# Gate and up projections of two feed-forward layers by Strassen's identity: seven half-size products in place of eight

## The chip, the cores and the metric

The kernel runs on one core of one Trainium2 chip. The metric is the device time of one execution, in microseconds. Before the change the median of three runs is 2283.34 us (2282.11 to 2284.97).

## What is computed

512 tokens of width 1024 pass through two blocks. The first is a mixer (mLSTM and a spatial gate) and a mixture of 32 experts. The second has two layers, each a mixer (HGRN2 in layer 0, dilated attention in layer 1) and a feed-forward part. The change is in the feed-forward part of both layers:

```python
D_FF = ((8 * D_MODEL // 3 + 255) // 256) * 256      # 2816, that is 22 chunks of 128

def swiglu_ffn(u, w_in, w_down):
    gate, up = jnp.split(u @ w_in, 2, axis=-1)
    return (jax.nn.silu(gate) * up) @ w_down

        h = h + swiglu_ffn(rmsnorm(h, norm_ffn[layer]), ffn_w_in[layer], ffn_w_down[layer])
```

## The kernel before

**Precision.** Every large product is made of three: a number is split into a high part (what the fp32r type keeps of it) and a low part (the rest), and `product` (L576 to L580) adds high x high, high x low and low x high in one bank of PSUM. ScalarE makes the high parts by a copy, VectorE the low parts by a subtraction.

**Weights.** They stream through SBUF in units of 1 MB (128 partitions x 2048 floats). SyncE loads them into four buffers `raw`, in order. For unit n ScalarE writes `w_hi[n % 2]` (`split`, L1310; in the loops L1568) and VectorE `w_lo[n % 2]` (L1808; in the loops L2240). A unit of the gate/up projections holds, for each of the 8 chunks of the model width, 128 gate columns and 128 up columns. A unit of the down projection holds 4 chunks of the hidden width x 512 output columns.

**A feed-forward layer.** The residual stream `hs` lies transposed: 8 row blocks of 128 model rows x 512 tokens. `u_hi`, `u_lo` are `hs` times the norm's gain; the factor 1/rms per token is applied to the results, as the tile `rms`. There are 22 gate/up units. After the first 12 (`FA`) come six units of the down projection (`out_rows`), then the other 10 gate/up units and again six down units (`out_rows`, in the last layer `last_rows`). For one gate/up unit (`unit` inside `ffn`):
- TensorE makes the gate into bank 2s and the up into bank 2s+1, s = n % 2, each with 8 x 3 products of 128x128 (weights, stationary) and 128x512 (moving).
- VectorE multiplies gate by rms (L2422), ScalarE takes the SiLU (L1680), GpSimd multiplies by rms again (L2714, that is for up), VectorE multiplies by the up bank (L2425: `f_hid`), ScalarE takes the high part (L1683) and VectorE the low part (L2428) of the hidden chunk.

**Order.** Each engine has one queue, which is written out by hand and runs in that order; semaphores join them. Most of a pass is in a loop of four units a trip. `add_rows` (VectorE) and `norm_rows` (ScalarE) stand between the stages: they add the eight banks of a down projection to `hs` as they become complete, and make `u_hi`, `u_lo` and the squares for the next norm; GpSimd sums the squares (`add_squares`).

Of the kernel before, what the change touches and what calls it, by code (L numbers as in the profile page):

```python
# [15 lines left out]
P = 128  # L16
# [6 lines left out]
HALF = D // 2  # L23
NG = 8
# [15 lines left out]
FA = 12  # L40
# [33 lines left out]
def columns(*sizes):  # L74
    at, out = 0, {}
    for name, n in sizes:
# [11 lines left out]
                        ("n_mix", 2 * KC), ("n_ffn", 2 * KC), ("lb", 3 * KC), ("og", 1), ("levels", 8 * P))  # L88
P3_LATE, P3_FIRST = P3_COLS["spare"][0], P3_COLS["n_mix"][0]
FIRST_LEVEL = 11  # L90

# [26 lines left out]
def build(nc, x_in, weights_in, constants_in, phase1_in, phase2_in, phase3_in, out):  # L118
    with ExitStack() as ctx:
# [149 lines left out]
        sq = [place(f"sq{n}", [T], at_b + (24 + n) * KB2) for n in range(2)]  # L269
        sq_acc = place("sq_acc", [T], at_b + 26 * KB2)  # L270
# [34 lines left out]
        f_hid = [place(f"f_hid{n}", [T], at_a2 + (6 + n) * KB2) for n in range(2)]  # L305

# [94 lines left out]
        PROJ_ATTN = 4 * (HH // 2) + FC  # L401
# [82 lines left out]
        fin_root, fin_ready = sem("fin_root"), sem("fin_ready")  # L484
        block = ctx.enter_context(nc.Block())
# [84 lines left out]
        def _(pe):  # L570
# [373 lines left out]
            def norm(k):  # L944

                pe.wait_ge(n_acc, 6 * k)
                nc.tensor.matmul(bank[4][:], ones, sq_acc[:], start=True, stop=False)
                pe.wait_ge(n_sq, KC * k)
                nc.tensor.matmul(bank[4][:], ones, sq[1][:], start=False, stop=True).then_inc(n_sum, 1)
# [6 lines left out]
            def out_rows(n0, n_chunks, source, ready=None, bank_free=None, between=None):  # L956
# [3 lines left out]
                for half in range(2):  # L960
                    for q in range(per_half):
                        n = n0 + half * per_half + q
                        unit_wait(n)
                        for d in range(4):
                            if bank_free is not None and half == 0 and q == 0:
                                bank_free(d)
                            for k in range(4 if q else lead):
# [5 lines left out]
                                mm = product(bank[4 * half + d][:], w_hi[:, n % 2, w], w_lo[:, n % 2, w], hi, lo,  # L973
# [161 lines left out]
            def ffn(l, u0):  # L1135

                def unit(n, done, i=None):

                    def at(v):
                        return v if i is None else i * 4 + v  # L1140
                    s = n % 2
                    pe.wait_ge(hi_ready, at(nth(n) + 1))
                    pe.wait_ge(lo_ready, at(nth(n) + 1))
                    if not (l == 0 and done < 2 and i is None):
                        pe.wait_ge(f_prod, at(done - 1))
                    feature_chunk(bank[2 * s][:], s, 0, 1 + 2 * l if n == u0 and i is None else None).then_inc(proj_ready, 1)
                    feature_chunk(bank[2 * s + 1][:], s, 1).then_inc(unit_used, 1)

# [9 lines left out]
                pe.wait_ge(h_added, 4 + 24 * l)  # L1158
                for j in range(4):
                    unit(u0 + j, base + j)  # L1160
                with pe.Fori(1, FA // 4) as i:
                    for j in range(4):
                        unit(u0 + j, base + j, i)
                out_rows(u0 + FA, FA, lambda c: (hid2_hi[:, c], hid2_lo[:, c]), hidden_ready(0),
                         lambda d: pe.wait_ge(f_prod, base + FA - 1 + d // 2))
                pe.wait_ge(h_added, 12 + 24 * l)
                u1 = u0 + FA + 6
                with pe.Fori(0, 2) as i:
                    for j in range(4):
                        unit(u1 + j, base + FA + j, i)  # L1170
                for j in range(8, FC - FA):
                    unit(u1 + j, base + FA + j)
                if l == 1:
                    last_rows(u1 + FC - FA, FC - FA, hidden_ready(FA), lambda b: pe.wait_ge(f_prod, base + FC - 1 + b // 2))
                    return
                out_rows(u1 + FC - FA, FC - FA, lambda c: (hid2_hi[:, c], hid2_lo[:, c]), hidden_ready(FA),
                         lambda d: pe.wait_ge(f_prod, base + FC - 1 + d // 2))

# [120 lines left out]
        def _(act):  # L1299
# [5 lines left out]
            def split(n):  # L1305

                act.wait_ge(raw_landed[n % RAW], (AFTER_MOE if n >= U_HG else 0) + 16 * (nth(n) // RAW + 1))
                if n >= 2:
                    act.wait_ge(unit_used, n - 1)
                nc.scalar.activation(w_hi[:, n % 2], raw[:, n % RAW], ACT.Copy).then_inc(hi_ready, 1)  # L1310
# [220 lines left out]
            def square(k, c, wait_chunk):  # L1531
# [6 lines left out]
                nc.scalar.activation(sq[c % 2][:], hs[:, c], ACT.Square).then_inc(n_sq, 1)  # L1538
# [25 lines left out]
            def split_trip(n, i, per):  # L1564

                act.wait_ge(raw_landed[n % RAW], i * (16 * per // RAW) + (AFTER_MOE + 16 * (nth(n) // RAW + 1)))
                act.wait_ge(unit_used, i * per + (n - 1))
                nc.scalar.activation(w_hi[:, n % 2], raw[:, n % RAW], ACT.Copy).then_inc(hi_ready, 1)  # L1568
# [94 lines left out]
            norm_rows(1, U_HGO, 2, g_ffn[:, 0:KC], 0, 1)  # L1663

            def ffn(l, u0):
                base = l * FC

                def unit(n, chunk, slot, i=None):

                    def at(v):  # L1670
                        return v if i is None else i * 4 + v
                    if i is None:
                        split(n + 1)
                    else:
                        split_trip(n + 1, i, 4)
                    s = n % 2
                    if chunk == base and i is None:
                        root(1 + 2 * l)
                    act.wait_ge(f_scaled, at(chunk + 1))
# [1231 lines left out]
```

## Time and profile before

| | |
|---|---|
| median of the runs | 2283.34 us |
| the profiled execution, its time | 2283.39 us |
| its span in the trace | 2281.7 us |
| busy: TensorE, VectorE, ScalarE, GpSimd | 2093.5, 905.9, 667.4, 381.2 us |
| gate/up stretches | 1207 to 1342, 1409 to 1522, 1830 to 1965, 2032 to 2145 us |
| granted TensorE clock, mean | 0.973 |

PE is TensorE, PEld its weight loads, DVE VectorE, ACT ScalarE, POOL GpSimd, SP SyncE. Matmul records overlap, since they are pipelined, so the sum of their durations is more than the time in which TensorE is busy. A line can be that of a helper: L578 to L580 stand for all products.

### The profile page before, as it was taken

Reading aid. Unit: us, or ns where it says so; the run is one execution under the profiler, and the core shown is the slowest. Engines: PE = TensorE matmul, PEld = TensorE weight load, DVE = VectorE, ACT = ScalarE, POOL = GpSimd, SP = SyncE. Lnnn points to the kernel's source line nnn. Section 1 sums busy time; section 2 is a strip of 40 time slices with the busy share of each in tenths; the row PEclk is TensorE's granted clock in tenths of the full one; section 3 lists DMA queues with packets and bytes.
Section 4 is the critical chain, followed back from the end, with each engine's and each line's share of the span. In section 5 each row is a group of like instructions: output and inputs, shape, how many; then the busy total and the mean of one; then the engine's idle time right before and its main releaser. Section 6 shows DMA issues by size and latency. Waiting matters only on the chain.

```text
span 2281.7 us, 26227 instructions
## 1 busy us (share of the span) xinstructions
PE 2093.5 (92%) x10354; PEld 1555.0 (68%) x10354; DVE 905.9 (40%) x1168; ACT 667.4 (29%) x851; POOL 381.2 (17%) x364
## 2 busy tenths in 40 slices
PE   6997968777787779999999999999999999999998
PEld 5895833232232348888777888877889987888887
DVE  5536340000000026777754333336766234333332
ACT  3434211100101016666533221223222423221222
POOL 0000320000000004545521100102444001100100
PEclk9998979999999999999999999999999999999999
DMA  5230379999999971111212222232222322222220
GB/s 206 78 108 1 122 303 420 421 421 421 421 421 421 421 324 67 64 56 59 91 44 93 92 92 92 92 111 92 83 87 91 130 93 77 98 102 92 92 92 37
DMA packets 57658, 378.13 MB, mean 166 GB/s; under 512 B 8960, under 2 KB 9056, under 8 KB 13920
## 3 DMA queue, kind: packets, MB, share of 16 engines
q1 hardware_dynamic: 51120, 363.04, 40.6%
q0 software_dynamic: 6448, 13.82, 1.6%
q8 instruction: 65, 1.06, 0.2%
q14 instruction: 25, 0.20, 0.0%
HBM read 371.01 MB, written 15.26 MB: 169 GB/s over the span
## 4 chain that ended last, share of the span: by engine, by line
PE 67%; DMA 18%; DVE 7%; issue 5%; ACT 2%; SPq 0%; POOL 0%; DVEq 0%; POOLq 0%
PE bank L578 19%; PE bank L580 19%; PE bank L579 19%; DMA moe_w<-weights_in 17%; PE bank L840 3%; PE bank L863 2%; DVE o_tmp L2330 1%; DVE k_dec L2306 1%; PE bank L936 1%; PE bank L1259 1%; PE bank L706 1%; PE bank L1037 1%; PE bank L1049 1%; DVE ws L2315 0%; PE bank L1207 0%
## 5 line engine op out<-in xcount | busy, mean ns | idle before, releaser
L578 PE MATMUL bank<-u_hi,w_hi 128*128 128x512 f32 x1152 | 464.7, 403 | 0.7 <-issue 0.7
L580 PE MATMUL bank<-u_hi,w_lo 128*128 128x512 f32 x1152 | 456.6, 396 | 0.0
L579 PE MATMUL bank<-u_lo,w_hi 128*128 128x512 f32 x1152 | 456.4, 396 | 0.0
L1808 DVE TENSOR_TENSOR w_lo<-raw,w_hi 128x2048 fp32r<-128x2048 f32 x96 | 232.6, 2423 | 301.6 <-ACT w_hi L1310 301.3
L840 PE MATMUL bank<-moe_w,xe 128*64 128x512 f32 x1088 | 266.9, 640 | 90.0 <-DMA moe_w<-weights_in 86.3
L840 PEld LDWEIGHTS bank<-moe_w,xe 128*64 128x64 f32 x1088 | 92.7, 146 | 263.3 <-issue 263.1
L1310 ACT ACTIVATE w_hi<-raw 128x2048 fp32r<-128x2048 f32 x96 | 183.6, 1912 | 273.8 <-PE bank L580 272.8
L578 PEld LDWEIGHTS bank<-u_hi,w_hi 128*128 128x128 f32 x1152 | 217.2, 189 | 53.9 <-issue 3.5
L579 PEld LDWEIGHTS bank<-u_lo,w_hi 128*128 128x128 f32 x1152 | 217.4, 189 | 53.1 <-issue 2.4
L580 PEld LDWEIGHTS bank<-u_hi,w_lo 128*128 128x128 f32 x1152 | 217.1, 188 | 52.8
L578 PE MATMUL bank<-w_hi,u_hi 128*128 128x256 f32 (+1 forms) x640 | 192.4, 301 | 6.8 <-issue 6.8
L580 PE MATMUL bank<-w_hi,u_lo 128*128 128x256 f32 (+1 forms) x640 | 189.3, 296 | 0.0
L579 PE MATMUL bank<-w_lo,u_hi 128*128 128x256 f32 (+1 forms) x640 | 188.2, 294 | 0.0
L2714 POOL TENSOR_TENSOR f_gate<-f_gate,rms 128x512 f32<-128x512 f32 x44 | 56.9, 1294 | 569.2 <-ACT f_gate L1680 569.2
L2179 DVE SCALAR_TENSOR_TENSOR hid<-bank,slot_scale,gate 128x512 f32<-128x512 f32 x16 | 12.0, 751 | 324.1 <-PE bank L840 324.1
L863 PE MATMUL bank<-moe_w,hid_t 128*64 128x512 f32 x544 | 123.3, 596 | 15.0 <-ACT hid_t L1467 9.8
L578 PEld LDWEIGHTS bank<-w_hi,u_hi 128*128 128x128 f32 x640 | 121.7, 190 | 10.9 <-issue 8.0
L579 PEld LDWEIGHTS bank<-w_lo,u_hi 128*128 128x128 f32 x640 | 122.5, 191 | 3.0
L580 PEld LDWEIGHTS bank<-w_hi,u_lo 128*128 128x128 f32 x640 | 121.0, 189 | 3.2
L2425 DVE TENSOR_TENSOR f_hid<-f_gate,bank 128x512 f32<-128x512 f32 x44 | 30.3, 688 | 213.7 <-PE bank L580 213.7
L578 PE MATMUL bank<-hid_hi,w_hi 128*128 128x512 f32 x272 | 107.9, 397 | 0.1
L580 PE MATMUL bank<-hid_hi,w_lo 128*128 128x512 f32 x272 | 107.8, 396 | 0.0
(434 smaller groups left out, 2800.4 us busy)
## 6 DMA issues: line engine op xcount, KB each, us to landing
moe_w<-weights_in SPq DMA_DIRECT2D x204, 1024.0 KB, 25.1
raw<-weights_in SPq DMA_DIRECT2D x128, 1024.0 KB, 4.8
y_pairs<-pair_rows SPq DMA_DIRECT2D x4, 1024.0 KB, 7.8
res<-x_in SPq DMA_DIRECT2D x1, 2048.0 KB, 7.8
token_rows<-xn POOLq DMA_DIRECT2D x4, 512.0 KB, 3.4
v_rows<-vals SPq DMA_DIRECT2D x2, 1024.0 KB, 4.3
vals<-v_rows SPq DMA_DIRECT2D x2, 1024.0 KB, 8.0
out<-out_tile SPq DMA_DIRECT2D x4, 512.0 KB, 2.6
```

The source lines that it names most:

```text
L578: nc.tensor.matmul(out_ap, a_hi, b_hi, start=first, stop=False)
L579: nc.tensor.matmul(out_ap, a_hi, b_lo, start=False, stop=False)
L580: return nc.tensor.matmul(out_ap, a_lo, b_hi, start=False, stop=last)
L706: mm = nc.tensor.matmul(bank[4 + b // 2][:, at:at + VH], dec_at(j, b * P, b * P + P), vm[:, j, h * VH:h * VH + VH], start=b % 2 == 0 and j ...
L840: mm = nc.tensor.matmul(bank[2 + j // 2][rows, :], xe[:, c, rows], moe_w[2 * j + b][:, w], start=c == 0, stop=c == KC - 1)
L863: mm = nc.tensor.matmul(bank[5 + half][rows, :], hid_t[:, c, rows], moe_w[2 * j + b][:, w], start=c == 0, stop=c == 3)
L936: mm = nc.tensor.matmul(of_block(c, b), y_pairs[b][:, k, c * P:c * P + P], share_diag[:, k, b], start=False, stop=b == TB - 1 and k == 1)
L1037: mm = nc.tensor.matmul(bank[4 + n % 2][:, t], left, right, start=True, stop=True)
L1310: nc.scalar.activation(w_hi[:, n % 2], raw[:, n % RAW], ACT.Copy).then_inc(hi_ready, 1)
L1808: nc.vector.tensor_tensor(w_lo[:, n % 2], raw[:, n % RAW], w_hi[:, n % 2].bitcast(F32), ALU.subtract) \
L2425: nc.vector.tensor_tensor(f_hid[s][:], f_gate[s][:], bank[2 * s + 1][:], ALU.mult).then_inc(f_prod, 1)
L2714: nc.gpsimd.tensor_tensor(f_gate[n][:], f_gate[n][:], rms[:], ALU.mult).then_inc(f_gated, 1)
```

## The change

With A the weights of one unit and B the activations, both are cut in four. A's halves are 512 of the 1024 model rows (second index) and gate or up columns (first index); B's are the same model rows (first index) and 256 of the 512 tokens (second index). The form used is Winograd's variant of Strassen's identity, with seven products and fifteen sums:

S1 = A21 + A22, S2 = S1 - A11, S3 = A11 - A21, S4 = A12 - S2;
T1 = B12 - B11, T2 = B22 - T1, T3 = B22 - B12, T4 = B21 - T2 up to sign;
P1 = A11 B11, P2 = A12 B21, P3 = S4 B22, P4 = A22 T4, P5 = S1 T1, P6 = S2 T2, P7 = S3 T3;
U2 = P1 + P6, U3 = U2 + P7, U4 = U2 + P5;
C11 = P1 + P2, C12 = U4 + P3 (gate), C21 = U3 + P4, C22 = U3 + P5 (up).

Each P is 4 x 3 matmuls of 128x128 by 128x256 in its own bank. GpSimd makes the S sums, VectorE the T sums (once a layer, `add_pairs`) and the C and U sums (each unit); ScalarE and VectorE split every part in high and low; ScalarE copies P1 and P5 to SBUF. Parts have one buffer each (`part_hi`, `part_lo`; the sums lie where their low parts go). The scaling of the gate by rms goes from VectorE to GpSimd. The 22 chunks are cut 11 and 11. A part of the parameters is loaded after the first layer's last gate/up unit and not during the last beats of HGRN2.

The core of the diff, one unit n in each engine's queue (waits are left out where only they are, and the helpers' bodies where a sentence above says them):

```diff
-FA = 12
+FA = 11
# TensorE
+                        if n == 0:
+                            p1()
+                            p5()
+                            p2()
+                            p6()
+                            if mixing:
+                                norm(1 + 2 * l)
+                            p7()
+                        elif n < FA:
+                            p1()
+                            p5()
+                            p4()
+                            p6()
+                            p3()
+                            p2()
+                            p7()
+                        else:
+                            p4()
+                            p3()
...
# ScalarE (take_high makes a high part)
+                    copy_p1()
+                    if not last:
+                        landed(unit, i)
+                        take_high("a11", quarter(unit, "a11")).then_inc(part_hi_ready, 1)
+                    copy_p5()
...
+                    used("p4", n - 1)
+                    take_high("a22", quarter(c.unit + n, "a22")).then_inc(part_hi_ready, 1)
+                    if not last:
+                        summed("s1", n + 1)
+                        take_high("s1", from_sum("s1")).then_inc(part_hi_ready, 1)
+                    if n >= 2:
+                        hid_high(n - 2, i)
+                    if last:
+                        out_piece(0, "p1")
+                        out_piece(1, "p5")
+                        out_piece(2, "p6")
                     else:
+                        used("p6", n)
+                        summed("s2", n + 1)
+                        take_high("s2", s2_sum[(n + 1) % 2][:]).then_inc(part_hi_ready, 1)
+                    act.wait_ge(unit_used, at(c.unit + n, 1))
+                    summed("s4", n)
+                    take_high("s4", from_sum("s4")).then_inc(hi_ready, 1)
+                    if last:
+                        out_piece(3, "p2")
+                    else:
+                        used("p2", n)
+                        take_high("a12", quarter(unit, "a12")).then_inc(part_hi_ready, 1)
+                    silu(n - 1, i)
+                    if not last:
+                        used("p7", n)
+                        summed("s3", n + 1)
+                        take_high("s3", from_sum("s3")).then_inc(part_hi_ready, 1)
...
# VectorE (low_x and take_low make a low part; product is gate x up)
+                    if n >= 2:
+                        was_added("c21", n - 2)
+                        product(n - 2, i)
+                    add_c21()
+                    high("a22", n)
+                    take_low("a22", quarter(c.unit + n, "a22")).then_inc(part_lo_ready, 1)
+                    if not last:
+                        low_s1()
+                    if n >= 2:
+                        hid_low(n - 2, i)
+                    add_u2()
+                    if not last:
+                        low_s2()
+                    else:
+                        out_piece(0)
+                        out_piece(1)
+                    add_c12()
+                    dve.wait_ge(hi_ready, at(nth(c.unit + n) + 1, 1))
+                    take_low("s4", from_sum("s4")).then_inc(lo_ready, 1)
+                    add_c11()
+                    if not last:
+                        low_a12()
+                    else:
+                        out_piece(2)
+                    add_u3()
+                    if not last:
+                        low_s3()
...
# GpSimd
+                    if not last:
+                        landed(c.unit + n + 1, i)
+                        pool.wait_ge(part_used, at(PART_USED + c.used("p5", n), 6))
+                        sum_s1(c.unit + n + 1)
+                        pool.wait_ge(sum_ready, at(SUM_READY + c.sum("s1", n + 1), 4))
...
+                        sum_s2(c.unit + n + 1, (n + 1) % 2)
+                    if n:
+                        scale(n - 1, i)
+                        pool.wait_ge(unit_used, at(c.unit + n, 1))
+                        pool.wait_ge(sum_ready, at(SUM_READY + c.sum("s2", n), 4))
+                        sum_s4(c.unit + n, n % 2)
+                        scale_again(n - 1, i)
+                    if not last:
+                        pool.wait_ge(part_used, at(PART_USED + c.used("p7", n), 6))
+                        sum_s3(c.unit + n + 1)
```

On VectorE the low of the next A11 stands first in the body (`low A11`). `add_u3` makes U3, then C22 and U4. Each `add_` of a P waits for that group; C12 also for U4, and U3 for U2. After the last body the order is: ScalarE high of the hidden, SiLU, high of the hidden; VectorE the product of chunk 9, C21, the last quarter of the first down unit's `w_lo` (`out_piece(3)`), C12, then lows and product of the last two chunks. At a layer's entry, for each of the row blocks 4 to 7, `add_pairs` does on VectorE: the addition to `hs`, T3, T2, `u_lo`, T4, low of T2, low of T3.

## Rows read from the trace of the kernel before

**Rows 1.** The page, parts 1 and 2: busy time, and 40 slices.
```profile
PE 2093.5 (92%) x10354; PEld 1555.0 (68%) x10354; DVE 905.9 (40%) x1168; ACT 667.4 (29%) x851; POOL 381.2 (17%) x364
PE   6997968777787779999999999999999999999998
PEclk9998979999999999999999999999999999999999
```
**Rows 2.** Windows of the first and last gate/up stretch: stretch, length, busy time of each engine, clock.
```profile
1207.00:1342.00 135.00, 135.00 (x575) 107.91 (x574) 54.97 (x48) 38.62 (x38) 15.53 (x12) 1.00 0.26 94
2032.00:2145.00 113.00, 113.00 (x484) 90.84 (x483) 36.56 (x30) 23.78 (x18) 5.18 (x4) 1.00 0.27 93
```
**Rows 3.** Timeline within a gate/up pass: start, duration, engine, line, operation.
```profile
1420.86 0.69 DVE L2425 TENSOR_TENSOR f_hid<-f_gate,bank 128x512 f32<-128x512 f32 x1 [4.93 <-PE bank L580]
1421.67 0.63 ACT L1683 ACTIVATE hid_hi<-f_hid 128x512 f32 x1 [5.08 <-DVE f_hid L2425]
1422.21 1.90 ACT L1568 ACTIVATE w_hi<-raw 128x2048 fp32r<-128x2048 f32 x1
1422.46 0.69 DVE L2428 TENSOR_TENSOR hid_lo<-f_hid,hid_hi 128x512 f32 x1 [0.91 <-ACT hid_hi L1683]
1426.48 0.69 DVE L2422 TENSOR_TENSOR f_gate<-bank,rms 128x512 f32<-128x512 f32 x1
1427.21 0.63 ACT L1680 ACTIVATE f_gate<-f_gate 128x512 f32<-128x512 f32 x1 [3.10 <-DVE f_gate L2422]
1427.92 1.30 POOL L2714 TENSOR_TENSOR f_gate<-f_gate,rms 128x512 f32<-128x512 f32 x1 [9.97 <-ACT f_gate L1680]
1432.11 0.69 DVE L2425 TENSOR_TENSOR f_hid<-f_gate,bank 128x512 f32<-128x512 f32 x1 [4.93 <-PE bank L580]
```
**Rows 4.** Windows: a stream of 256-column products, and one of 512.
```profile
116.00:126.00 10.00, 10.00 (x85) 10.00 (x85) 2.29 (x1) 3.00 (x3) 0.00 (x0) 1.00 0.34 117
1420.00:1430.00 10.00, 10.00 (x44) 8.06 (x43) 4.36 (x4) 3.07 (x3) 1.30 (x1) 1.00 0.22 79
```
**Rows 5.** Groups of the stretch 1130 to 1560: count, busy us, mean ns, idle before.
```profile
L2422 DVE TENSOR_TENSOR f_gate<-bank,rms 128x512 f32<-128x512 f32 x22 | 15.2, 692 | 2.4 <-PE bank L580 1.4
L2259 DVE SCALAR_TENSOR_TENSOR u_lo<-hs,par,u_hi 128x512 fp32r<-128x512 f32 x12 | 11.1, 924 | 7.9 <-ACT u_hi L1545 7.9
L1680 ACT ACTIVATE f_gate<-f_gate 128x512 f32<-128x512 f32 x22 | 13.9, 632 | 70.0 <-DVE f_gate L2422 70.0
L2714 POOL TENSOR_TENSOR f_gate<-f_gate,rms 128x512 f32<-128x512 f32 x22 | 28.5, 1294 | 284.6 <-ACT f_gate L1680 284.6
```
**Rows 6.** Groups of 256 columns, one on VectorE, one on ScalarE.
```profile
L2480 DVE TENSOR_TENSOR prob<-bank,par 128x256 f32<-128x256 f32 x4 | 1.7, 420 | 6.5 <-PE bank L1204 6.5
L1588 ACT ACTIVATE ws<-bank 128x256 f32<-128x256 f32 x1 | 0.4, 386 | 0.2 <-PE bank L1021 0.2
```
**Rows 7.** Timeline of VectorE and GpSimd in the attention stage.
```profile
1591.57 1.30 POOL L2725 TENSOR_TENSOR q_rot<-r_cos,r_sin 128x512 f32<-128x512 f32 x1 [12.32 <-DVE r_sin L2468]
1592.25 0.69 DVE L2467 TENSOR_TENSOR r_sin<-bank,par 64x512 f32<-64x512 f32 x1
1593.72 1.29 POOL L2725 TENSOR_TENSOR q_rot<-r_cos,r_sin 128x512 f32<-128x512 f32 x1 [0.85 <-DVE r_sin L2468]
1593.75 3.41 DVE L1808 TENSOR_TENSOR w_lo<-raw,w_hi 128x2048 fp32r<-128x2048 f32 x1
1605.45 2.29 DVE L1808 TENSOR_TENSOR w_lo<-raw,w_hi 128x2048 fp32r<-128x2048 f32 x1
1605.50 3.39 POOL L2725 TENSOR_TENSOR k_rot<-r_cos,r_sin 128x512 f32<-128x512 f32 x1 [4.33 <-DVE r_sin L2468]
1758.03 11.77 DVE L1808 TENSOR_TENSOR w_lo<-raw,w_hi 128x2048 fp32r<-128x2048 f32 x1 [7.63 <-ACT w_hi L1310]
1760.15 7.49 POOL L2762 TENSOR_TENSOR prob<-prob,share_turned 128x1024 f32<-128x1024 f32 x4
```
**Rows 8.** Window of an early stretch in which TensorE pauses at times.
```profile
285.00:342.00 57.00, 39.63 (x189) 21.27 (x188) 23.54 (x85) 7.27 (x15) 13.74 (x14) 0.76 0.77 302
```

More of the change, by code:

```diff
@@ L972, in out_rows @@
                                 hi, lo = source(c)
-                                mm = product(bank[4 * half + d][:], w_hi[:, n % 2, w], w_lo[:, n % 2, w], hi, lo,
+                                mm = product(bank[4 * half + d][:], w_hi[:, side(n), w], w_lo[:, side(n), w], hi, lo,
                                              c == 0, c == n_chunks - 1)
@@ L1135, in ffn @@
             def ffn(l, u0):
[L1137 to L1147, printed above, removed]
                 base = l * FC
@@ new lines, in evacuated, with wait @@
+                def evacuated(c):
+                    def wait(d):
+                        if d == 0:
+                            pe.wait_ge(copied, COPIED + c.copy("p5", FA - 1))
+                        pe.wait_ge(added, ADDED + c.add(("c11", "u3", "c21", "c12")[d], FA - 1))
+                    return wait
+                hid = lambda c: (hid2_hi[:, c], hid2_lo[:, c])
+                one, two = Pass(l, 0), Pass(l, 1)
+                gate_up(one)
+                out_rows(one.unit + FA, FA, hid, hidden_ready(0), bank_free=evacuated(one))
@@ L1693, in ffn @@
                 with act.Fori(0, 2) as i:
                     for j in range(4):
-                        unit(u1 + j, base + FA + j, j, i)
-                for j in range(8, FC - FA):
-                    unit(u1 + j, base + FA + j, j)
+                        body(2 + j, i)
+                body(FA - 1)
+                hid_high(FA - 2)
+                silu(FA - 1)
+                hid_high(FA - 1)
+            def ffn(l, u0):
+                one, two = Pass(l, 0), Pass(l, 1)
+                gate_up(one)
+                for n in range(one.unit + FA + 1, two.unit):
+                    split(n)
+                first_parts(two)
+                second_parts(two)
+                gate_up(two)
@@ L2275, in add_rows @@
                     low(c)
+                if then is not None:
+                    second_parts(then)
             def inverse_root(k):
@@ L2439, in ffn @@
                 with dve.Fori(0, 2) as i:
                     for j in range(4):
-                        unit(u1 + j, base + FA + j, j, i)
-                for j in range(8, FC - FA):
-                    unit(u1 + j, base + FA + j, j)
+                        body(2 + j, i)
+                body(FA - 1)
+                product(FA - 2)
+                body(FA)
+                hid_low(FA - 2)
+                product(FA - 1)
+                hid_low(FA - 1)
+            def ffn(l, u0):
+                one, two = Pass(l, 0), Pass(l, 1)
+                gate_up(one)
+                add_rows(one.unit + FA, 3, 6 + 18 * l, then=two)
+                gate_up(two)
```

640 lines of the change are left out of this document (521 added, 119 removed).

## The prediction

> **What bounds the kernel now.** The page's first two parts come first: TensorE is busy for 2093.5 of 2281.7 us, the others for 40, 29 and 17%, and in slices 22 to 39, which hold both feed-forward layers, its digit is 9 at full granted clock [rows 1]. The stage windows say the same without rounding: in the first and the last of the four gate/up stretches TensorE is busy for all of the 135 and 113 us (the two between, as long, show the same), while VectorE works 55 and 37 us of them and GpSimd 16 and 5 [rows 2]. So here TensorE alone sets the time, and each of the 44 units (a pair of 128 gate and 128 up columns) costs 48 products of 512 columns: the two f_hid operations of neighbouring units start 11.25 us apart [rows 3], which is 234 ns a product (a record lasts 396 ns, but they overlap). 44 units make 495 us.
>
> **What the change takes off TensorE.** Each unit becomes seven groups of 12 products of 256 columns, 84 in place of 48. What such a product costs must be read as a rate: between 116 and 126 us a stream of nothing but 128x256 products passes 85 in 10 us, while 44 of 512 columns pass in 10 us of the gate/up stage [rows 4]; without the edges 0.120 and 0.234 us. A unit is then 84 x 0.120 = 10.08 us, 1.17 less; over 44 units 51.5 us. The eighth saved would be 61.9, but the half-size product takes 3 ns more than half. That is all that can be won; the down projections keep their 22 chunks per layer, split 11/11 in place of 12/10, still three weight units a half, so they cost the same.
>
> **What it adds elsewhere, per unit.** ScalarE: seven high parts of 512 columns, a SiLU, a high part of the hidden, and copies of P1 and P5 (256): 9 x 0.632 + 2 x 0.386 = 6.5 us [rows 5, 6]. VectorE: seven low parts, the product with up, the low of the hidden (9 x 0.692 [rows 5]) and seven half-size additions (0.42 each [rows 6]): 9.2 us. GpSimd: four sums of weights and two scalings by rms, 6 x 1.296 [rows 5] = 7.8 us. Each alone fits in 10.08 us. What doesn't fit is their combination, for two reasons.
>
> **First: VectorE and GpSimd exclude each other.** The w_lo operation (two inputs in SBUF) takes 2.29 us; started 0.03 us after a GpSimd operation it takes 3.41 and ends 2.15 us after that one's end. Turned round, a GpSimd operation started 0.05 us after a w_lo takes 3.39 in place of 1.30 and ends 1.15 us after the w_lo. And a w_lo issued in a run of GpSimd operations lasts 11.77 us, ending 2.16 us after the last of them [rows 7]. Additions from a PSUM bank (r_cos, r_sin) run beside GpSimd at their usual 0.69 [rows 7]. So the exclusive time is 1.15 us for a GpSimd operation and, with 1.04 ns a column (2.29 less 0.69 over 1536 columns), 0.55 for a VectorE one of 512 and 0.28 for one of 256. Before, a unit had one GpSimd operation with VectorE idle under it [rows 3]. After, GpSimd's six, the seven lows, the product and the hidden's low, and of the additions C22 and U4 (both inputs in SBUF) need it: 6 x 1.15 + 9 x 0.55 + 2 x 0.28 = 12.4 us a unit. That is above 10.08, and above the old 11.25.
>
> The Trainium skill has this as a rule (SBUF — State Buffer, "Who interferes with whom"): a VectorE instruction with two SBUF inputs and a GpSimd one that reads SBUF block each other for a whole instruction, and whoever issued first has it. The trace agrees with 3.41 and 3.39 us, but the 11.77 us show more: the waiting one isn't served between two queued GpSimd operations. By the page's rule C22 and U4 would get in before GpSimd's fourth sum, by the row after it; in the schedule below that is 0.4 us a unit, some 15 in all.
>
> **Second: the queues form a loop.** Each engine runs its written order, so I follow one turn, from VectorE's C12 of unit n-1 to C12 of unit n, with the durations of [rows 5, 6], hand-offs of 0.04 to 0.1 us (f_gate: VectorE ends 1427.17, ScalarE starts 1427.21, ends 1427.84, GpSimd starts 1427.92 [rows 3]), and 0.05 to 0.09 us of overlap of neighbours on one engine (ScalarE's w_hi starts 0.09 before hid_hi ends [rows 3]):
> C12 0 to 0.43; GpSimd scales f_gate to 1.8 and only then, next in its queue, makes S4, to 3.0; ScalarE's high of S4 to 3.7, high of A12, then SiLU, to 4.8; meanwhile VectorE does low S4, C11, low A12, to 5.4, which holds GpSimd's second scaling (ready 4.9) back to 5.4, so it ends at 6.7; behind it in the queue S3, to 8.0; ScalarE's high of S3, copy of P1, high of the next A11, to 9.5. On VectorE, U3 ran to 5.8, but C22 and U4 wait for the exclusive resource, to 8.7; GpSimd's next S1 to 10.0; VectorE low S3, low A11, product, C21, to 12.3, with S2 squeezed in from 11.95 to 13.25; then low A22, low S1, low of the hidden, U2, low S2, to 16.2, where C12 starts again.
> The same chain with no blocking at all adds up to 13.7. So a unit takes 16.2 us, of which TensorE needs 10.08; its groups wait, but none is on the loop (the nearest, P3, ends near 6 and is wanted at 16.2). Ends of this term: 13.7 below, and 17.5 above (no overlap of neighbours, and 0.05 us more for each of some 18 instructions on the loop that has two or three waits: f_hid to hid_low took 0.15 where a register had to be worked out first [rows 3]).
>
> **A pass of 11 units.** Start: TensorE's first seven groups need only first parts, but unit 1's lows come after the copies, P5 and three sums: low S1 near 6.5, low S3 near 10.6, first C12 at 15.5 us. Then nine turns, the last of them 2 us lighter (quarters of the down unit replace the next unit's parts, and no S1 and S2). End: scale, S4, high, low, P3 would be 6.0 us after the last C12 of the loop, but the last quarter of the down unit's w_lo stands on VectorE behind the product with up, which waits for SiLU and the second scaling: 8.6. A pass is 15.5 + 9 T - 2 + 8.6 = 22.1 + 9 T. With T = 16.2 it is 167.9 us, four are 671.6, against 495: +176.6.
>
> **Entry of each layer.** add_pairs does, for each of the last four row blocks, the addition (0.69), a u_lo (0.92 [rows 5]; it shares with GpSimd's squares) and five half-width operations of 0.42, 3.7 us, up to 5 with the square beside it, where rows come 2.8 us apart (12 products of 0.234). The fourth is ready some 10 to 11 us after the last row, TensorE covers 2.9 with P1 and P5, and P2, P6 and P7 end about 5 us late. Before, TensorE had no such gap [rows 2]. Twice: +10, between 0 (hidden by the start of a pass, which waits for other parts anyway) and +20. The DMAs stay as many; the late parameter load moves behind the first layer's gate/up units, some 67 us before rope uses it: nothing, or its own few us if not. Unit loads come four units ahead: nothing.
>
> **Sum.** The profiled execution took 2283.39 us (span 2281.7), the median is 2283.34, so nothing is to be converted. 2283.4 + 176.6 + 10 = 2470 us.
>
> **Rivals.**
> A. TensorE stays the bound, and the kernel gets faster: the loop is cut because a part is ready a unit earlier than I read it, and exclusion is weaker than the three cases show. For it: every engine's own sum is under 10.08. Against it: the 12.4 us. Then 44 x 10.08 plus some 4 x 3 of pass ends and 10 of entries: -51.5 + 22 = -30, 2254 us. It decides from a turn of 11.0 us: 4 x (22.1 + 9 T - 123.75) + 10 = 0.
> B. The queues overlap so well that blocking falls into waits: T is the bare loop, 13.7. 4 x (22.1 + 123.3 - 123.75) + 10 = +97, 2380 us. For it: VectorE is idle while GpSimd scales and makes S4. Against: 12.4 of 13.7 would have to be used without a hole.
> C. A turn over 17.5 us: GpSimd's run delays VectorE further, or TensorE, now 60% busy with pauses, is granted a lower clock. In an early stretch with TensorE busy 39.6 of 57 us, 70%, the clock was 0.76 [rows 8]. At 0.8 a unit is 12.6 us, still off the loop; at half clock it would be 20.2, and bind: 4 x (9 x 4) = +144 more, 2614 us. Between the forecast's upper end and that I take 2560 us.
> D. The operations cost as counted but TensorE's lead hides the turn, giving a turn near 11: about 2283 us.
>
> **How the numbers follow.** Forecast 0.73 (turns of 14.5 to 17.5, 2409 to 2517 us), A 0.05, B 0.12, C 0.08, D 0.02. Range 2370 to 2540: it holds the forecast, B and the near part of C. About 0.2% tells a change from none here: faster 0.05, same 0.02, slower 0.93.
>
> **What would show it.** The 256-column products stay at 0.12 us apart inside a group, with pauses before groups put down to VectorE's part_lo; U2 or C12 of neighbouring units lie 15 to 17.5 us apart; low parts' mean is well over 0.69 and GpSimd's sums well over 1.30, while C11, U2, U3 stay near 0.42; TensorE's digits in the gate/up slices fall to 6. I am wrong if the turn is under 14 us, if the blocked operations keep their undisturbed means, or if TensorE is busy throughout these stretches.

## The result, and the profile after

The changed kernel takes 2467.78 us (median of 4 runs, 2463.74 to 2468.78) against 2282.73 us (4 runs of the kernel before on the same chip): ratio 1.0809, interval 1.079 to 1.0827. The forecast was 2470 us. The profiled execution took 2463.74 us, its span is 2462.0 us.

The first two parts of the page, which answer to [rows 1]:

```profile
PE 2106.7 (86%) x11938; PEld 1644.5 (67%) x11938; DVE 1228.0 (50%) x1760; ACT 791.9 (32%) x1243; POOL 703.7 (29%) x584
...
PE   6997887777877799998877897799999987799779
...
PEclk9998889999999999999999999999999999999999
```

In the gate/up slices TensorE's digit falls from 9 to 7 and 8. The stage windows (columns as in [rows 2]) of the four passes and of one turn of the loop:

```profile
1204.40:1379.80 175.40, 133.14 (x929) 126.18 (x927) 132.75 (x194) 67.95 (x133) 91.59 (x64) 0.89 0.19 66
1442.90:1603.40 160.50, 125.10 (x926) 119.55 (x925) 120.77 (x174) 60.43 (x119) 89.36 (x62) 0.93 0.20 72
1986.20:2162.90 176.70, 130.91 (x930) 123.61 (x928) 132.78 (x194) 69.17 (x134) 91.57 (x64) 0.91 0.19 66
2226.90:2387.30 160.40, 124.90 (x926) 119.32 (x924) 120.68 (x174) 60.42 (x119) 89.34 (x62) 0.94 0.20 73
...
1490.00:1505.18 15.18, 11.48 (x82) 11.05 (x82) 11.34 (x17) 5.55 (x11) 8.68 (x6) 0.89 0.20 70
```

The passes take 673.0 us where 44 units took 495: +178.0 of the 180.3 by which the span grew. The two passes that begin a layer are 15 to 16 us longer than the others. In a turn no engine is busy throughout: VectorE 11.34, TensorE 11.48 and GpSimd 8.68 of 15.18 us. That looks like a loop of waits, which the experiments below test. The turn itself, VectorE and GpSimd, from one C12 (L2945) to the next (L2590 makes the low parts, L3298 S4, L3294 S3, L3286 S1, L3290 S2; L3322 and L3328 scale the gate):

```profile
1490.70 0.41 DVE L2945 TENSOR_TENSOR f_gate<-bank,f_u 128x256 f32<-128x256 f32 x1
1494.41 0.69 DVE L2590 TENSOR_TENSOR part_lo<-part_sum,part_hi 128x512 fp32r<-128x512 f32 x1 [3.30 <-ACT part_hi L1775]
1495.35 0.68 DVE L2590 TENSOR_TENSOR part_lo<-raw,part_hi 128x512 fp32r<-128x512 f32 x1
1496.49 0.98 DVE L2934 TENSOR_TENSOR f_hid<-f_u,f_p 128x256 f32<-128x256 f32 x1
1497.39 1.51 DVE L2935 TENSOR_TENSOR f_u<-f_u,f_p 128x256 f32<-128x256 f32 x1
1499.31 1.26 DVE L2590 TENSOR_TENSOR part_lo<-part_sum,part_hi 128x512 fp32r<-128x512 f32 x1 [0.42 <-ACT part_hi L1775]
1500.50 1.77 DVE L2590 TENSOR_TENSOR part_lo<-raw,part_hi 128x512 fp32r<-128x512 f32 x1
1502.19 0.68 DVE L2858 TENSOR_TENSOR f_hid<-f_gate,f_hid 128x512 f32<-128x512 f32 x1
1502.79 0.41 DVE L2940 TENSOR_TENSOR f_hid<-bank,f_u 128x256 f32<-128x256 f32 x1
1505.86 0.41 DVE L2945 TENSOR_TENSOR f_gate<-bank,f_u 128x256 f32<-128x256 f32 x1
```
```profile
1491.19 1.29 POOL L3322 TENSOR_TENSOR f_gate<-f_gate,rms 128x512 f32<-128x512 f32 x1 [4.63 <-DVE f_gate L2945]
1492.43 1.29 POOL L3298 TENSOR_TENSOR part_sum<-raw,s_sum 128x512 f32<-128x512 f32 x1
1495.49 1.69 POOL L3328 TENSOR_TENSOR f_gate<-f_gate,rms 128x512 f32<-128x512 f32 x1 [1.78 <-ACT f_gate L1946]
1497.15 1.47 POOL L3294 TENSOR_TENSOR part_sum<-raw 128x512 f32<-128x512 f32 x1
1498.58 1.45 POOL L3286 TENSOR_TENSOR part_sum<-raw 128x512 f32<-128x512 f32 x1
1500.10 1.62 POOL L3290 TENSOR_TENSOR s_sum<-part_sum,raw 128x512 f32<-128x512 f32 x1
```

Read the two together. C22 (L2934) is issued while GpSimd scales for the second time, and ends 0.29 us after that ends at 1497.18. GpSimd's S3, issued next, is held up in turn and takes 1.47 us in place of 1.29. U4 (L2935) ends 0.28 us after S3, and so on: each engine is served behind one operation of the other. Additions with a bank as input (C11, U2, U3, C12: 0.41 us) are not touched. TensorE's main wait in the stretch 1250 to 1372 (us in total, times, longest), and groups of VectorE in it (count, busy us, mean ns):

```profile
PE bank L685 <- DVE part_lo L2590: 25.6, 17, 2.3
```
```profile
L2590 DVE TENSOR_TENSOR part_lo<-raw,part_hi 128x512 fp32r<-128x512 f32 x23 | 23.3, 1011 | 0.0
L2935 DVE TENSOR_TENSOR f_u<-f_u,f_p 128x256 f32<-128x256 f32 x8 | 12.0, 1506 | 0.0
...
L2926 DVE TENSOR_TENSOR f_u<-bank,f_p 128x256 f32<-128x256 f32 x9 | 3.7, 410 | 0.0
```

### The profile page after: what moved, and what is told of

It is laid out like the page before. It is cut to its first block, busy times and chain, and to the rows that moved or that the text cites. A ratio compares the mean times of both kernels' runs of the same rounds, so it can differ in the third digit from the quotient of the medians.

```text
span 2462.0 us, 32292 instructions
## 1 busy us (share of the span) xinstructions
PE 2106.7 (86%) x11938; PEld 1644.5 (67%) x11938; DVE 1228.0 (50%) x1760; ACT 791.9 (32%) x1243; POOL 703.7 (29%) x584
## 4 chain that ended last, share of the span: by engine, by line
PE 42%; issue 18%; DMA 17%; POOL 10%; DVE 10%; ACT 3%; SPq 0%; POOLq 0%; DVEq 0%; ACTq 0%
DMA moe_w<-weights_in 16%; PE bank L685 11%; PE bank L686 11%; PE bank L687 11%; PE bank L947 3%; POOL s_sum L3290 2%; POOL part_sum L3294 2%; POOL part_sum L3286 2%; POOL part_sum L3298 2%; PE bank L970 1%; DVE o_tmp L2773 1%; DVE w_lo L2158 1%; DVE k_dec L2749 1%; PE bank L1043 1%; PE bank L1463 1%
## 5 line engine op out<-in xcount | busy, mean ns | idle before, releaser
L685 PE MATMUL bank<-t_hi,part_hi 128*128 128x256 f32 x704 | 214.1, 304 | 90.2 <-DVE part_lo L2590 85.7
L685 PEld LDWEIGHTS bank<-t_hi,part_hi 128*128 128x128 f32 x704 | 142.6, 203 | 101.2 <-issue 91.8
L687 PE MATMUL bank<-t_hi,part_lo 128*128 128x256 f32 x704 | 207.9, 295 | 0.0
L686 PE MATMUL bank<-t_lo,part_hi 128*128 128x256 f32 x704 | 207.6, 295 | 0.0
L2590 DVE TENSOR_TENSOR part_lo<-part_sum,part_hi 128x512 fp32r<-128x512 f32 x132 | 111.3, 843 | 164.0 <-ACT part_hi L1775 156.2
L1775 ACT ACTIVATE part_hi<-part_sum 128x512 fp32r<-128x512 f32 x132 | 83.1, 630 | 339.4 <-POOL part_sum L3298 185.1
L685 PE MATMUL bank<-u_hi,w_hi 128*128 128x512 f32 x448 | 184.8, 412 | 0.7 <-issue 0.7
L687 PE MATMUL bank<-u_hi,w_lo 128*128 128x512 f32 x448 | 177.7, 397 | 0.0
L686 PE MATMUL bank<-u_lo,w_hi 128*128 128x512 f32 x448 | 177.4, 396 | 0.0
L2590 DVE TENSOR_TENSOR part_lo<-raw,part_hi 128x512 fp32r<-128x512 f32 x132 | 131.8, 999 | 24.6 <-ACT part_hi L1775 24.6
L686 PEld LDWEIGHTS bank<-t_lo,part_hi 128*128 128x128 f32 x704 | 143.4, 204 | 0.5 <-issue 0.5
L687 PEld LDWEIGHTS bank<-t_hi,part_lo 128*128 128x128 f32 x704 | 143.3, 204 | 0.0
```

Of the source, the lines that this page charges most:

```text
L685: nc.tensor.matmul(out_ap, a_hi, b_hi, start=first, stop=False)
L686: nc.tensor.matmul(out_ap, a_hi, b_lo, start=False, stop=False)
L687: return nc.tensor.matmul(out_ap, a_lo, b_hi, start=False, stop=last)
L1775: return nc.scalar.activation(part_hi[:, PARTS.index(name)], src, ACT.Copy)
L2590: return nc.vector.tensor_tensor(part_lo[:, i], src, part_hi[:, i].bitcast(F32), ALU.subtract)
```

## Experiments on the turn of the loop

A turn is the time from one C12 to the next. Theory: two things hold it at 15.18 us, the exclusion of VectorE and GpSimd and the loop of hand-offs through GpSimd's second scaling and S4. Rival: the loop alone, with blocked operations falling into time in which the engine would have waited anyway. So the loop was loosened alone, the exclusion weakened alone, and both at once.

**Looser loop (`orders`, and half of it, `again_later`).** On GpSimd:

```diff
                     last = n == FA - 1
+                    if n >= 2:
+                        scale_again(n - 2, i)
                     if not last:
                         landed(c.unit + n + 1, i)
...
                         sum_s4(c.unit + n, n % 2)
-                        scale_again(n - 1, i)
...
                 body(FA - 1)
+                scale_again(FA - 2)
                 scale(FA - 1)
```

`orders` also puts ScalarE's high of S4 behind SiLU, and VectorE's low of S4 behind U3.

> Nothing is left out; only the order in the queues changes. GpSimd does the second scaling of a unit's gate one body later (at the start of the body, where its SiLU is long done) and so makes S3 right behind S4, and ScalarE and VectorE make the parts of S4 behind A12, the SiLU and U3. That cuts the loop from C12 over scaling, S4, SiLU, second scaling and S3 back to C12. If the loop alone sets the turn of 15.18 us, it falls by the second scaling, S3 and the wait for high S4, to 11.0 to 12.4 us, and the time by 32 looped turns x 3 or more, to under 2370 us. If the exclusion of VectorE and GpSimd sets it, each of GpSimd's six operations still holds VectorE up for about 1.1 us beside its own 7.8 us of work: turn 14.0 to 14.7 us, time 2435 to 2455 us. If neither, 15.2 us and no change.

> One order alone: GpSimd's second scaling (scale_again) stands one body later, so that it follows a gate chunk that has long been ready; the high and low parts of S4 stay where they are. If the turn was set by exclusion together with the loop over that scaling (my account of the turn of 15.18 us), the loop loses the wait for SiLU and the turn falls to about 14.5 us, 9 turns x 4 passes x 0.65 = 23 us less: about 2440 to 2450 us. If all of the 1.34 us that the two changed orders gave came from this one, the turn is 13.8 and the time about 2418. If it all came from S4's place, the turn stays at 15.2 and the time at 2465.

**Fewer operations that exclude each other (`one_input`), and both (`one_input_orders`).** `in_loop` is true in the looped bodies, 2 to 9 of each pass.

```diff
+                if in_loop[0]:
+                    with nc.allow_low_precision(reason="one input"):
+                        return nc.vector.tensor_reduce(part_lo[:, i], part_hi[:, i].bitcast(F32).unsqueeze(3), AX.X, ALU.add)
                 return nc.vector.tensor_tensor(part_lo[:, i], src, part_hi[:, i].bitcast(F32), ALU.subtract)
```

> In the looped bodies (2 to 9 of each pass) the low parts of the weights are made by an operation with one SBUF input (a reduction over an axis of length one, same 512 columns), so they are no longer source minus high part; its part of the arithmetic is left out. Queues and waits are those of the changed kernel. If exclusion with GpSimd needs two SBUF inputs, the seven lows stop being blocked and stop blocking: second scaling, S3, S1 and S2 take near 1.30 us, the turn is that of the bare loop, 13.1 to 13.9 us, time 2410 to 2430 us. If GpSimd slows for another reason (any VectorE activity), they keep 1.45 to 1.69 us and the turn 15.2.

> Both edits together: low parts of the looped bodies with one SBUF input (their arithmetic left out) and the changed orders. With the loop cut and the exclusion mostly gone, VectorE has 7.8 us of work and at most four blocked operations, TensorE 10.08 us: turn 10.1 to 11.5 us, time 2305 to 2350 us. If loop and exclusion did not each hold the turn up, it would equal the better of the two single runs.

**Parts almost free (`small_parts`).** In the looped bodies `cut` shortens every sum, high and low part to 8 of each 128 columns:

```diff
+        def cut(ap):
+            return ap[:, :, 0:8] if in_loop[0] else ap
...
-                return nc.vector.tensor_tensor(part_lo[:, i], src, part_hi[:, i].bitcast(F32), ALU.subtract)
+                return nc.vector.tensor_tensor(cut(part_lo[:, i]), cut(src), cut(part_hi[:, i].bitcast(F32)), ALU.subtract)
```

> In the looped bodies the sums, high and low parts of the weights are made for 32 of 512 columns only (the rest of the parts stays that of an earlier unit); all products, waits and queues stay. This shows TensorE's own rate in the new form, with all its waits. By the term of the prediction a turn is 84 x 0.120 = 10.08 us, up to 10.3 if the waits on TensorE cost something, and the time falls by 32 x 5.1 = 163 to about 2305 us. If TensorE's clock or its waits were a limit of their own, the turn would stay over 11 us.

The turn can be read off one row each, the line of C12 in steady turns of the second pass: count, shortest/median/longest ns, start of the first and of the last. After, `again_later`, `orders`, `one_input`, `one_input_orders`, `small_parts`:

```profile
L2945 DVE TENSOR_TENSOR f_gate<-bank,f_u x8: 407/410/411, 1475.5 to 1581.7; 128x256 f32<-128x256 f32 x8
```
```profile
L2945 DVE TENSOR_TENSOR f_gate<-bank,f_u x7: 408/409/409, 1481.2 to 1566.9; 128x256 f32<-128x256 f32 x7
```
```profile
L2950 DVE TENSOR_TENSOR f_gate<-bank,f_u x8: 409/409/411, 1465.2 to 1562.1; 128x256 f32<-128x256 f32 x8
```
```profile
L2949 DVE TENSOR_TENSOR f_gate<-bank,f_u x7: 404/406/409, 1481.0 to 1564.1; 128x256 f32<-128x256 f32 x7
```
```profile
L2954 DVE TENSOR_TENSOR f_gate<-bank,f_u x6: 413/416/418, 1450.8 to 1505.9; 128x256 f32<-128x256 f32 x6
```
```profile
L2951 DVE TENSOR_TENSOR f_gate<-bank,f_u x4: 424/425/425, 1462.1 to 1492.0; 128x256 f32<-128x256 f32 x4
```

Each ratio is to the kernel before as it ran beside that kernel (medians of 2280.24 to 2282.73 us), in this table and the next.

| kernel | median us | ratio to before | turn, us |
|---|---|---|---|
| after | 2467.78 | 1.0809 [1.079, 1.0827] | 106.2 / 7 = 15.17 |
| again_later | 2435.06 | 1.0674 [1.0655, 1.0694] | 85.7 / 6 = 14.28 |
| orders | 2416.44 | 1.0588 [1.0557, 1.0618] | 96.9 / 7 = 13.84 |
| one_input | 2428.75 | 1.0642 [1.0611, 1.0673] | 83.1 / 6 = 13.85 |
| one_input_orders | 2327.75 | 1.0199 [1.017, 1.0229] | 55.1 / 5 = 11.02 |
| small_parts | 2283.65 | 1.0012 [1.0001, 1.0023] | 29.9 / 3 = 9.97 |

Loosening the loop alone gives 1.33 us, weakening the exclusion alone 1.32, and both 4.15, more than the sum. So the rival falls: if the loop alone set the turn, `orders` would have gone below 12.4. What stopped it at 13.84 is a VectorE that is working or blocked for 69.39 of 70 us, with its low parts at twice their length; with one input they go back to 677 ns beside the same GpSimd. I had expected 14.0 to 14.7 us and 2435 to 2455 for that case, so `orders` gained more than I had put on it. Window and two groups of `orders`, then a group of `one_input` and the window of `one_input_orders`, 1260 to 1330:

```profile
1260.00:1330.00 70.00, 56.24 (x420) 55.24 (x420) 69.39 (x81) 29.92 (x59) 46.44 (x32) 0.90 0.20 75
```
```profile
L2595 DVE TENSOR_TENSOR part_lo<-part_sum,part_hi 128x512 fp32r<-128x512 f32 x16 | 22.4, 1424 | 0.0
L2595 DVE TENSOR_TENSOR part_lo<-raw,part_hi 128x512 fp32r<-128x512 f32 x15 | 20.6, 1370 | 0.0
```
```profile
L2593 DVE TENSOR_REDUCE part_lo<-part_hi 128x512 fp32r<-128x512 f32 x35 | 23.3, 677 | 19.2 <-ACT part_hi L1776 18.6
```
```profile
1260.00:1330.00 70.00, 64.87 (x539) 63.67 (x538) 67.47 (x105) 36.50 (x69) 51.54 (x38) 1.00 0.25 92
```

`one_input` weakens the exclusion and does not remove it: U4 (mean 1513 ns) and the product with up (1248) are still blocked, and S1 and S3 still take 1.45 and 1.48 us, where I had expected 1.30. With both edits VectorE is again working or blocked for 67.47 of 70 us, so the 11.02 us are still above TensorE's 9.9.

`again_later` shows how the two changed orders share the gain: 0.89 us from GpSimd's, and 0.44 from S4's on top of it (S4's alone was not run). I had put 0.65 on the first. `small_parts` reaches TensorE's own bound, and still the kernel is not faster than before. Its steady turns take 9.86 to 9.97 us. My expectation of some 2305 us was 21 too high, since I priced eight turns a pass at 5.1 us less each; the first turn (12.1 to 13.1 us) and the last (10.4) shrink too, and two or three behind the first take 8.2 to 9.8, less than TensorE's 9.9: there VectorE catches up. Its passes (111 to 129 us from the first to the last product of parts) begin with the same 17 us to the first C12, or 31 and 33 at a layer's entry, as all others and end with 19 us for the last two turns; these eat what the seven products save. No version tried beats the kernel before; of those that do the whole computation `orders` is the fastest, 2416.44 us.

## Experiments on the entry of a layer

The first C12 comes 31.5 and 32.8 us after the start of a layer's first pass, and 17.3 and 17.2 after that of its second: 14 and 16 us where I had put 5. Rows of the first entry, VectorE, GpSimd, then TensorE's two long pauses (each the only row of its stretch with one):

```profile
1205.20 1.51 DVE L2659 SCALAR_TENSOR_TENSOR t_sum<-hs,par,t_sum 128x256 f32<-128x256 f32 x1
...
1207.49 0.68 DVE L2626 TENSOR_TENSOR hs<-bank,hs 128x512 f32<-128x512 f32 x1
...
1212.59 1.48 DVE L2664 TENSOR_TENSOR t_lo<-t_sum,t_hi 128x256 fp32r<-128x256 f32 x1
1214.00 0.68 DVE L2626 TENSOR_TENSOR hs<-bank,hs 128x512 f32<-128x512 f32 x1
...
1216.81 0.74 DVE L2656 SCALAR_TENSOR_TENSOR u_lo<-hs,par,u_hi 128x512 fp32r<-128x512 f32 x1
...
1227.56 3.35 DVE L2723 RECIPROCAL rms<-rms 128x512 f32<-128x512 f32 x1
```
```profile
1205.00 1.43 POOL L3273 TENSOR_TENSOR sq_acc<-sq_acc,sq 128x512 f32<-128x512 f32 x1 [3.11 <-ACT sq L1742]
...
1230.98 1.61 POOL L3286 TENSOR_TENSOR part_sum<-raw 128x512 f32<-128x512 f32 x1 [4.79 <-DVE rms L2723]
```
```profile
1208.28 0.47 PE L685 MATMUL bank<-t_hi,part_hi 128*128 128x256 f32 x1 [2.25 <-issue]
```
```profile
1217.61 0.58 PE L685 MATMUL bank<-u_hi,part_hi 128*128 128x256 f32 x1 [5.09 <-DVE u_lo L2656]
```

VectorE has no pause from these rows to the end of the reciprocal. Three suspects stand there: T4 (L2659), blocked by GpSimd's squares for 1 us in each of the first three row blocks; GpSimd's weight sums under the third and fourth; and the reciprocal, which ends the norm and for which the next S1 waits. I had not counted the last at all. (S1 waits by the order of GpSimd's queue, `pool.wait_ge(rms_ready, ...)` at the end of its first body; the first operation that reads `rms` is the scaling behind S1 and S2. Moving that wait was not tried.) The first and the last were taken away, singly and together:

```diff
-                        nc.gpsimd.tensor_tensor(sq_acc[:], sq_acc[:], sq[c % 2][:], ALU.add).then_inc(n_acc, 1)
+                        w = slice(0, 8) if k % 2 and c >= 4 else slice(0, T)
+                        nc.gpsimd.tensor_tensor(sq_acc[:, w], sq_acc[:, w], sq[c % 2][:, w], ALU.add).then_inc(n_acc, 1)
...
+                if k % 2:
+                    return nc.vector.tensor_scalar(rms[:], rms[:], 0.0, 0.3, ALU.mult, ALU.add)
                 return nc.vector.reciprocal(rms[:], rms[:])
```

> The reciprocal that ends the norm of each feed-forward layer (3.35 us on VectorE) is replaced by writing the constant 0.3 (about 0.7 us); 1/rms is left out of the result. If the reciprocal is on the path that sets the first C12 of a layer, that C12 starts 2.5 us earlier after the start of the stretch (28.9 in place of 31.5 us) in both layers: 5 us less, 2463. If the late lows and sums of the last row blocks set it alone, nothing changes (2468). Turns inside the passes stay at 15.2.

> GpSimd's additions of the squares of the last four row blocks of each feed-forward norm are done on 8 of 512 columns; the rest of that sum is left out of the result. If exclusion between these and VectorE's work on a row block makes the entry late, each of the four blocks takes some 0.5 to 1 us less, u_lo of the last one ends 2 to 4 us earlier and so does the first C12: 4 to 8 us less in all, 2460 to 2464. If GpSimd's weight sums are what VectorE meets there, or VectorE's own count of operations, it gains under 2 us.

> Both: the reciprocal replaced by a constant, and the squares of the last four row blocks on 8 of 512 columns. If the two costs stand one behind the other (first the rows' work, then the reciprocal), the gains add: 9 to 13 us less, 2455 to 2459, first C12 at 25 to 27 us after the start of the stretch. If they are parallel, it gives no more than the better of the two alone.

| kernel | start to first C12, first and third pass, us | median us | ratio to before |
|---|---|---|---|
| after | 31.5, 32.8 | 2467.78 | 1.0809 [1.079, 1.0827] |
| small_reciprocal | 28.9, 30.0 | 2461.04 | 1.0784 [1.0763, 1.0804] |
| small_squares | 28.5, 29.6 | 2457.49 | 1.0766 [1.0745, 1.0786] |
| small_both | 25.4, 26.7 | 2456.56 | 1.0767 [1.0749, 1.0785] |

For after and for `small_both`, the pass's first product and the line of the first two C12:

```profile
1204.44 0.28 PE L685 MATMUL bank<-b_hi,part_hi 128*128 128x256 f32 x1
```
```profile
L2945 DVE TENSOR_TENSOR f_gate<-bank,f_u x2: 409/412/414, 1235.9 to 1251.9; 128x256 f32<-128x256 f32 x2
```
```profile
1204.32 0.28 PE L685 MATMUL bank<-b_hi,part_hi 128*128 128x256 f32 x1
```
```profile
L2947 DVE TENSOR_TENSOR f_gate<-bank,f_u x2: 408/409/410, 1229.7 to 1245.7; 128x256 f32<-128x256 f32 x2
```

In the traces the reciprocal costs 2.6 and 2.8 us a layer and the squares 3.0 and 3.2, and they add up: 5.6 and 6.0 singly, 6.1 us together in either layer. They stand one behind the other. The medians don't resolve this: their intervals overlap, and that of `small_both` shows no gain over `small_squares`. Of the times that I expected, that of `small_squares` (2460 to 2464 us) was missed by 2.5. Executions also differ elsewhere by as much: the first pass starts between 1204.3 and 1205.4 us in these traces and at 1210.1 in that of `waits_between` below, whose edit comes only after it. The 8.1 and 9.5 us that are left against a second pass were not tried. In the trace they lie with the third row block's bank, which TensorE waits for (2.25 us), and with VectorE's row work: in `small_both` the first two blocks take 3.5 us each, where blocks come 2.8 us apart, and the last two, under GpSimd's weight sums, 5.5 and 4.7. So the weight sums, the third suspect, stand there with some 3 us that no run has taken away.

## Experiments on who is served when two engines want the same

In the loop VectorE is served between two GpSimd operations. In the attention stage of both kernels a w_lo waits through seven: the one under way, two more like it, and the four in the last line of [rows 7]. That difference was to be explained, with kernels that touch that place alone. The first puts a fulfilled wait before each GpSimd operation:

```diff
                 pr = prob_of(g, h)
+                pool.wait_ge(share_ready, 3)
```

> A wait that has long been fulfilled (for VectorE's shares, before the first of them) stands before each of GpSimd's twelve multiplications of the attention's probabilities. If what kept the w_lo operation of 11.77 us from being served was that GpSimd's operations stood with no wait between them, it is now served after the GpSimd operation under way: 2.3 to 4.5 us, and one of GpSimd's shows about 2 us more. If a waiting VectorE operation isn't served between queued GpSimd operations at all, which is how I read it for the prediction, it stays at 11.8. The time of the whole is that of the changed kernel in either case, 2463 to 2470 us.

The second makes `w_lo` there in four operations of 512 columns, the third gives GpSimd a plain second input (`nc.gpsimd.tensor_tensor(pr, pr, pr, ALU.mult)`), the fourth puts three waits before each.

> In the attention stage each w_lo of 2048 columns is made by four VectorE operations of 512 columns; nothing is left out. It asks whether the length of the waiting operation made the 11.77 us. If VectorE, once it waits, is never served while GpSimd's operations follow each other there, the first of the four lasts some 10 us and the others 0.6 each. If a short operation is served between two of GpSimd's, as C22 is in the loop of the feed-forward layer, each of the four takes 1.3 to 2.5 us and GpSimd's show about half a microsecond more each. The time of the whole doesn't move (2463 to 2470 us).

> GpSimd's twelve multiplications of the attention's probabilities take the probabilities themselves as second input and not one value spread over the columns; the shares are left out of the result. If it was this operand that kept the w_lo operation waiting through seven of them, it is now served after the one under way, 3 to 5 us in place of 11.77. If not, it ends about 2.2 us after GpSimd's last one again (over 11 us). The time of the whole doesn't move (2463 to 2470 us).

> Three waits on three different semaphores, all long fulfilled, stand before each of GpSimd's twelve multiplications of the attention's probabilities; nothing is left out. With no wait or with one, these operations follow each other 1.02 us apart (4.08 us for four of 512 columns) and w_lo waits through all of them; in the loop of the feed-forward layer the sums, which have several waits each, take 1.29 us and VectorE is served between them. If it is a gap of some tens of nanoseconds that the further waits make, the operations are now 1.05 us or more apart and w_lo is served after the one under way, in 2.3 to 5 us. If the number of waits doesn't matter either, it stays at 11.8 us. The time of the whole doesn't move (2463 to 2470 us).

The VectorE row of each, in this order (for `in_four` the first of its four operations; all four take 12.16 us):

```profile
1853.04 11.77 DVE L2158 TENSOR_TENSOR w_lo<-raw,w_hi 128x2048 fp32r<-128x2048 f32 x1 [7.63 <-ACT w_hi L1514]
```
```profile
1847.80 10.35 DVE L3121 TENSOR_TENSOR w_lo<-raw,w_hi 128x512 fp32r<-128x512 f32 x1 [7.43 <-ACT w_hi L1514]
```
```profile
1846.29 11.62 DVE L2158 TENSOR_TENSOR w_lo<-raw,w_hi 128x2048 fp32r<-128x2048 f32 x1 [7.64 <-ACT w_hi L1514]
```
```profile
1848.27 11.73 DVE L2158 TENSOR_TENSOR w_lo<-raw,w_hi 128x2048 fp32r<-128x2048 f32 x1 [7.64 <-ACT w_hi L1514]
```

None of the four differences decides by itself: not a wait, not three, not the length of the waiting operation, not the spread operand. The times of the whole were 2468.17, 2463.27, 2464.42 and 2463.60 us (the last three are single runs), in the 2463 to 2470 expected. What makes the one place take turns and the other not stays open. One difference was not tried: GpSimd's operations of 512 columns last 1.29 us in the loop and start 1.24 apart (1491.19, 1492.43), in the attention stage four take 4.08 us, 1.02 each.

## Why the prediction was right

The forecast of 2470 us was right in direction, and its two causes, exclusion and loop, hold. That the size was so near is luck: two errors of 38 and 31 us cancelled. Point by point:

- **The turn of the loop** was put at 16.2 us and is 15.2. The failed step is "the waiting one isn't served between two queued GpSimd operations". I followed the queues with it and held C22 and U4 to 8.7 us after C12; they end at 6.8 and 8.2, C22 0.29 us behind the second scaling and U4 0.28 behind S3. S2 then runs at 9.4 (1500.10) and not squeezed in at 11.95, so it no longer holds the low of A22. From C21's end (12.5; forecast 12.3) the last five operations take 2.7 us in place of 3.9: 0.9 of that is S2, 0.3 that neighbours on VectorE start 0.60 us apart where I took 0.65 (some 10 us over all turns, which have nothing to do with who is served). Over the nine turns of a pass it is 134.4 us measured (15.25 + 7 x 15.18 + 12.91) against 143.8; -38 us in all, where I had priced the question at 15. The Trainium skill (SBUF — State Buffer, "Who interferes with whom") lets the two engines block each other for one whole instruction, and whoever issued first has it; the loop goes by that rule, the attention stage doesn't.
- **Exclusion, and its prices**: right, though the rows of r_cos and r_sin, which I called additions, are multiplications from a bank; that additions from a bank are not blocked is seen in the changed kernel (0.41 us). Ends of blocked operations lie 0.28 (256 columns) and 0.55 us (512) behind GpSimd's: low A11 ends at 1502.27, S2 at 1501.72. Both parts of the cause, exclusion and loop, were needed, as `orders` and `one_input` show.
- **Start of a pass**: 15.5, measured 17.3; +7 us over four. In the first body of a pass, C22 and U4 meet the next unit's S1 and S2 and take 1.29 and 1.51 us (second pass), and the low of S3 comes at 13.6 us in place of 10.6.
- **End of a pass**: 8.6, measured 8.57 and 0.2 to the down projection.
- **Entry of a layer**: put at 5, measured 14.9 and 16.3 us (a later first C12, and a first turn of 15.97 in place of 15.25); +21 us over two. The reciprocal was left out (2.7 us each). The first two row blocks take 4.54 us, within my 3.7 to 5, but the third took 6.5 under GpSimd's weight sums, and I had not seen that P5, too, waits for a row block. TensorE also came out of these pauses at a lower clock.
- **TensorE**: 10.08 us a unit counted, 9.86 to 9.97 where it is the bound.
- **Signs**: turn, low parts and GpSimd's sums came as said (15.2 us; means of 853 and 1011 ns; 1.45 to 1.62 us for three of the four sums), but TensorE's digit fell to 7, not 6.
- **Moved load, unit loads, down projections**: nothing, as far as the span shows; 2.3 us of its growth lie outside the passes and are not assigned.

Pass by pass: forecast 671.6 + 10 for the entries, measured 673.0, of which -38 is the turns, +7 the starts, +1 the ends, +21 the entries; with 2.3 elsewhere 2463.7 us in place of 2470. Had the turn alone been right, the forecast would have been 2432 us, some 32 below the profiled execution.

Rival B (2380) fell because the loop alone is not the bound; rival A (2254) because the turn is 15.2 us, and even with parts almost free (`small_parts`) starts, ends and entries leave 2284; C's lower clock is there (0.89 to 0.94 in the passes), but in the loop TensorE has room for it. At the entries it was not tried.

## What to carry to other kernels

A saving on the busiest engine is worth what the others' added work leaves of it. Add up per unit, beside each engine's time, the time of whatever two engines can't use at once, and follow one turn through all queues; here the sums per engine (10.1, 9.2, 7.8, 6.5 us) all fitted under 11.25 and the turn took 15.2. Where a bound of contention and a loop of hand-offs lie close together, relieving one can give little and both much (here 1.3, 1.3 and 4.15 us of 15.2). And price starts, ends and entries of a pipelined stage: in `small_parts`, whose steady turn was 9.9 us, they cost the whole gain.

## What the runs showed of the hardware

- VectorE with one SBUF input (TENSOR_REDUCE, 512 columns) keeps its 677 ns beside GpSimd; with two it took up to 1424 in the mean.
- After pauses TensorE's clock was down at the entry of a layer: two windows there

```profile
1208.00:1212.00 4.00, 3.72 (x18) 3.75 (x19) 3.83 (x6) 1.86 (x4) 2.47 (x2) 0.57 0.01 4
1217.00:1224.00 7.00, 6.39 (x26) 5.16 (x27) 6.90 (x13) 5.77 (x12) 0.00 (x0) 0.64 0.31 95
```

  follow the pauses of 2.25 and 5.09 us; at 0.57, near the lower of its two levels (1.2 GHz), 18 products took 3.72 us, 0.207 each, against 0.12. The slow products of the first window end before the pause of 5.09 us, a wait for VectorE, so they hold no later product up.
- 256-column products pass 87 in 10 us in `small_parts`, where 85 passed in the stream of [rows 4] (84 in a turn of 9.86 us are 0.117 us each):

```profile
1290.00:1300.00 10.00, 10.00 (x87) 10.00 (x87) 6.07 (x17) 3.17 (x12) 4.12 (x7) 1.00 0.31 111
```
